# Attention scores as fp32r products over 128 rows of split queries and keys, and attention units in the order of heads

## The reference

```python
def diff_attend(q, k, v, lam):
    s = jnp.einsum('bhjqd,bhjkd->bhjqk', q, k).astype(jnp.float32) * (DA_HALF ** -0.5)
    p = jax.nn.softmax(s, axis=-1)
    w = p[:, :, 0] - lam * p[:, :, 1]
    return jnp.einsum('bhqk,bhkd->bhqd', w.astype(v.dtype), v)
...
    q_l = apply_rope(da_heads(dq), cos, sin)
    k_l = apply_rope(da_heads(dk), cos, sin)
    k_all = jnp.concatenate([k_l, k_c], axis=3)
```

## Time and profile before

| | |
|---|---|
| median of 3 runs | 2370.67 us (2369.45 to 2372.53) |
| profiled execution, its own time | 2370.8 us |
| its span, first to last instruction | 2369.0 us |
| TensorE busy | 2342.1 us, 99% of the span |
| VectorE busy | 1600.7 us, 68% |
| ScalarE busy | 978.1 us, 41% |
| mean granted TensorE clock | 0.999 |

### The profile page before, as it was taken

The page is one execution under the profiler, slowest core; times in us unless marked ns, Lnnn a source line. Parts: engine busy times, 40 slices in busy tenths (PEclk is TensorE's granted clock), DMA queues, the critical chain, the costliest instruction groups (busy, mean ns, idle before and its releaser), DMA issues.

```text
span 2369.0 us, 35156 instructions
## 1 busy us (share of the span) xinstructions
PE 2342.1 (99%) x12814; PEld 2014.8 (85%) x12814; DVE 1600.7 (68%) x2635; ACT 978.1 (41%) x1625; POOL 197.7 (8%) x186
## 2 busy tenths in 40 slices
PE   8999999999999999999999999999999999999998
PEld 5888889887887778898888898888898888999997
DVE  6998577456546445569885367887665756668876
ACT  5423224434345334363322254232245346555554
POOL 2111000000000000031111000211100000001220
PEclk9999999999999999999999999999999999999999
DMA  8888464232222322327883337775644433556654
GB/s 275 244 249 241 126 209 143 81 98 72 72 63 80 90 80 65 113 83 238 247 243 120 96 85 231 236 237 179 185 116 116 116 98 107 161 137 198 191 162 140
DMA packets 540054, 356.86 MB, mean 151 GB/s; under 512 B 15206, under 2 KB 490896, under 8 KB 539920
## 3 DMA queue, kind: packets, MB, share of 16 engines
q1 hardware_dynamic: 538472, 354.70, 51.0%
q10 hardware_dynamic: 1448, 0.38, 0.1%
HBM read 337.20 MB, written 17.83 MB: 150 GB/s over the span
## 4 chain that ended last, share of the span: by engine, by line
PE 91%; DVE 3%; ACT 2%; issue 2%; DMA 1%; SPq 1%; POOL 0%; DVEq 0%; ACTq 0%; POOLq 0%
PE ps L1015 25%; PE ps L1017 24%; PE ps L1016 24%; PE ps L1380 2%; PE ps L1314 2%; PE ps L1315 2%; PE ps L1313 2%; PE ps L1028 1%; PE ps L1395 1%; PE ps L1107 1%; PE ps L1109 1%; PE ps L1108 1%; PE ps L1356 1%; PE ps L1412 1%; PE ps L1030 1%
## 5 line engine op out<-in xcount | busy, mean ns | idle before, releaser
L2176 DVE TENSOR_TENSOR w_lo<-raw,w_hi 128x1024 fp32r<-128x1024 f32 (+3 forms) x430 | 496.2, 1155 | 480.0 <-ACT w_hi L1518 475.5
L1518 ACT ACTIVATE w_hi<-raw 128x1024 fp32r<-128x1024 f32 (+3 forms) x430 | 423.3, 985 | 895.6 <-PE ps L1017 714.1
L1015 PE MATMUL ps<-u_hi,w_hi 128*128 128x512 f32 (+2 forms) x2176 | 782.2, 359 | 1.7 <-DVE dav L2776 1.0
L1017 PE MATMUL ps<-u_hi,w_lo 128*128 128x512 f32 (+2 forms) x2176 | 772.6, 355 | 0.0
L1016 PE MATMUL ps<-u_lo,w_hi 128*128 128x512 f32 (+2 forms) x2176 | 772.3, 355 | 0.0
L1015 PEld LDWEIGHTS ps<-u_hi,w_hi 128*128 128x128 f32 x2176 | 410.9, 189 | 60.9 <-DVE dav L2776 1.8
L1017 PEld LDWEIGHTS ps<-u_hi,w_lo 128*128 128x128 f32 x2176 | 410.8, 189 | 58.2
L1016 PEld LDWEIGHTS ps<-u_lo,w_hi 128*128 128x128 f32 x2176 | 411.1, 189 | 55.9
L2592 DVE SCALAR_TENSOR_TENSOR ada_acc<-ada_in_up,cs,ada_acc 128x512 f32<-128x512 f32 x378 | 282.1, 808 | 0.0
L1015 PE MATMUL ps<-g,w_hi 128*128 128x512 f32 (+1 forms) x572 | 206.7, 361 | 0.0
L1017 PE MATMUL ps<-g,w_lo 128*128 128x512 f32 (+1 forms) x572 | 203.8, 356 | 0.0
(11 more groups left out here) (334 smaller groups left out, 3467.6 us busy)
## 6 DMA issues: line engine op xcount, KB each, us to landing
raw<-in_ffn_up SPq DMA_DIRECT2D x150, 512.0 KB, 4.7
raw<-in_w_in SPq DMA_DIRECT2D x132, 512.0 KB, 3.8
ada_in_up<-in_w_ada SPq DMA_DIRECT2D x108, 512.0 KB, 4.5
raw<-in_ffn_down SPq DMA_DIRECT2D x67, 384.0 KB, 3.3
fold_out<-ada_acc SPq DMA_DIRECT2D x32, 512.0 KB, 3.4
fold<-fold_out SPq DMA_DIRECT2D x32, 512.0 KB, 5.5
raw<-in_ffn_down SPq DMA_DIRECT2D x42, 320.0 KB, 3.1
h<-in_ffn_up SPq DMA_DIRECT2D x22, 512.0 KB, 4.5
```

Of the source, the lines that this page charges most:

```text
L1015: pe.matmul(ps[bank][:, cols_of], wh, a_hi, start=a, stop=False)
L1017: m = pe.matmul(ps[bank][:, cols_of], wl, a_hi, start=False, stop=b)
L1518: act.activation(hi, whole, ACT.Copy).then_inc(hi_done, 1)
L2176: dve.tensor_tensor(lo, whole, hi.bitcast(F32), ALU.subtract).then_inc(lo_done, 1)
```

## The change

The kernel after keeps, for one head at a time, split queries `qs` and keys `ks`. `qs[:, j, 0]` has the high part of half j's queries twice, in rows 0 to 63 and again in rows 64 to 127; `qs[:, j, 1]` the low part, twice. `ks[:, j]` has the high part of half j's keys in the 64 rows where they lie in `dqk` and their low part in the other 64. A score is then two fp32r products over 128 rows, accumulated in PSUM: high queries by both parts of the keys, low queries by both parts. To make these, ScalarE does 4 casts for a head's queries (`queries_high`) and 2 for its keys (`keys_high`), VectorE 4 and 2 subtractions (`queries_low`, `keys_low`), each over 64 partitions. The units go head by head, so that `qs` and `ks` can be written once for each head; the writes for the next head wait for the last scores of the one before (`head_free`). Head 0's queries are split in `proj_order` behind `ysplit` 5, its keys at the list's end, behind the last `dav`, because `ks` lies in the memory of `value_bias`.

```diff
-    order += [("dv", 1), ("rope", 3), ("rope", 7), ("ysplit", 4), ("ysplit", 5)]
+    order += [("dv", 1), ("rope", 3), ("rope", 7), ("ysplit", 4), ("ysplit", 5), ("queries", 0)]
     order += [("dv", 2), ("ysplit", 6), ("ysplit", 7), ("dv", 3)]
...
-    return [(head, t, range(2 if t < 2 else 4)) for t in tiles for head in range(HEADS)], 16 * layer
+    return [(head, t, range(2 if t < 2 else 4)) for head in range(HEADS) for t in tiles], 16 * layer
...
+    qs = at("qs", [P, 2, 2, TOK], F32R, 1152)
+    ks = at("ks", [P, 2, TOK], F32R, 1152 + 8192)
...
-            if v < HEADS:
-
-                pe.wait_ge(rope_done, 8 * layer + 2 * (head + 1))
+            if v % units_of_head(layer) == 0:
+                pe.wait_ge(q_ready, HEADS * layer + head + 1)
+                pe.wait_ge(k_ready, HEADS * layer + head + 1)
...
             for j in range(2):
-                half = slice(j * DA_HALF, (j + 1) * DA_HALF)
-                pe.matmul(ps[SCORE_BANK + j][:, 0:len(keys) * P], dqk[half, head, t * P:(t + 1) * P],
-                          dqk[half, 4 + head, 0:len(keys) * P], start=True, stop=True).then_inc(sc_ready, 1)
+                out, moving = ps[SCORE_BANK + j][:, 0:len(keys) * P], ks[:, j, 0:len(keys) * P]
+                pe.matmul(out, qs[:, j, 0, t * P:(t + 1) * P], moving, start=True, stop=False)
+                pe.matmul(out, qs[:, j, 1, t * P:(t + 1) * P], moving, start=False, stop=True).then_inc(sc_ready, 1)
...
+        def queries_high(layer, head):
+
+            t = slice(t0_of(layer), TOK)
+            act.wait_ge(rope_done, 8 * layer + 2 * (head + 1))
+            head_free(act, layer, head)
+            for j, own in enumerate(HALF_ROWS):
+                for rows_of in HALF_ROWS:
+                    m = act.activation(qs[rows_of, j, 0, t], dqk[own, head, t], ACT.Copy)
+            m.then_inc(q_high, 1)
+
+        def keys_high(layer, head):
+
+            if head == 0:
+                act.wait_ge(evac_dve, BASES[layer, "proj"][2] + PLANS[layer]["dv", 3][3] + 1)
+            head_free(act, layer, head)
+            for j, own in enumerate(HALF_ROWS):
+                m = act.activation(ks[own, j, :], dqk[own, 4 + head, :], ACT.Copy)
+            m.then_inc(k_high, 1)
...
+                    if step[0] == "scores" and next_head(layer, step[1]):
+                        queries_high(layer, next_head(layer, step[1]))
+                        keys_high(layer, next_head(layer, step[1]))
...
+        def queries_low(layer, head):
+
+            t = slice(t0_of(layer), TOK)
+            dve.wait_ge(rope_done, 8 * layer + 2 * (head + 1))
+            dve.wait_ge(q_high, HEADS * layer + head + 1)
+            for j, own in enumerate(HALF_ROWS):
+                for rows_of in HALF_ROWS:
+                    m = dve.tensor_tensor(qs[rows_of, j, 1, t], dqk[own, head, t], qs[own, j, 0, t].bitcast(F32),
+                                          ALU.subtract)
+            m.then_inc(q_ready, 1)
...
                     outputs(layer, step[1])
+                    if next_head(layer, step[1] + 1):
+                        queries_low(layer, next_head(layer, step[1] + 1))
+                        keys_low(layer, next_head(layer, step[1] + 1))
```

More of the change, by code:

```diff
@@ L245, in attention_units, with units_of_head, next_head @@
     tiles = range(2 if layer == DEPTH - 1 else 0, TT)
-    return [(head, t, range(2 if t < 2 else 4)) for t in tiles for head in range(HEADS)], 16 * layer
+    return [(head, t, range(2 if t < 2 else 4)) for head in range(HEADS) for t in tiles], 16 * layer
+def units_of_head(layer):
+    return len(attention_units(layer)[0]) // HEADS
+def next_head(layer, v):
+    n = units_of_head(layer)
+    return (v + 1) // n if (v + 1) % n == 0 and v + 1 < HEADS * n else None
 def gate_order(layer):
@@ L600, in build @@
     ng_split = sem("ng_split")
+    q_high, q_ready, k_high, k_ready = (sem(n) for n in ("q_high", "q_ready", "k_high", "k_ready"))
     ng_ready, s_ready, e_ready, pw_ready = (sem(n) for n in ("ng_ready", "s_ready", "e_ready", "pw_ready"))
@@ L667, in u32_of, with head_free @@
         return u32(n, ITEM_OF[k])[:, k % 2 * SEG:(k % 2 + 1) * SEG]
+    HALF_ROWS = (slice(0, DA_HALF), slice(DA_HALF, P))
+    def head_free(eng, layer, head):
+        if head:
+            units, u0 = attention_units(layer)
+            eng.wait_ge(sc_ready, 2 * (u0 + units_of_head(layer) * head))
+        else:
+            eng.wait_ge(ada_turned, (ADA_OF[1, "up0"] if layer else ADA_OF[0, "up1"]) - 4 +
+                        (ADA_UP + ADA_DOWN[1] if layer else 0))
     def run(eng, count, body, peel_first=False, peel_last=False):
@@ L888, in mixer @@
                         sp.wait_ge(*proj_done(layer - 1, CH_PROJ - 1))
+                        sp.wait_ge(sc_ready, 2 * len(attention_units(layer - 1)[0]))
                     for kind, n in (("mv", 2), ("dv", 1)):
@@ L1970, in mixer @@
                     split_y(y_number(layer, "mo", step[1]), ht[:, step[1], :], yml_hi, step[1], t0)
+                elif step[0] == "queries":
+                    queries_high(layer, 0)
+            keys_high(layer, 0)
             for step in GATE_ORDERS[layer]:
@@ L2879, in ml_numerator, with keys_low @@
                                      ALU.mult, ALU.add).then_inc(hsum_ready, 1)
+        def queries_low(layer, head):
[7 more added lines that the diff above has]
+            m.then_inc(q_ready, 1)
+        def keys_low(layer, head):
+            dve.wait_ge(k_high, HEADS * layer + head + 1)
+            for j, own in enumerate(HALF_ROWS):
+                m = dve.tensor_tensor(ks[HALF_ROWS[1 - j], j, :], dqk[own, 4 + head, :], ks[own, j, :].bitcast(F32),
+                                      ALU.subtract)
+            m.then_inc(k_ready, 1)
         def maxima(layer, v):
@@ L2990, in mixer @@
                     split_y(y_number(layer, "mo", step[1]), ht[:, step[1], :], yml_hi, yml_lo, step[1], t0)
+                elif step[0] == "queries":
+                    queries_low(layer, 0)
                 elif step[0] == "gates":
@@ L2996, in mixer @@
                     rope(layer, step[1])
+            keys_low(layer, 0)
             for step in GATE_ORDERS[layer]:
```

## The result

The changed kernel takes 2392.22 us (median of five runs, 2390.32 to 2395.49) beside 2370.9 us for the kernel before (five runs, 2369.45 to 2372.53): 0.91% slower, ratio 1.0091 with a 95% interval of 1.008 to 1.0102. The forecast was 2384 us. The measured time is 8.2 us above it and 1.2 us above the upper end of the range. The profiled execution of the changed kernel has 2390.67 us of its own and a span of 2388.9 us, 19.9 us more than before in both.

The account below looks back on a forecast made before the run. TensorE, busy 99% of the span, was taken to bound the kernel: -8.1 us from products, +13.5 at changes of head, +7.9 at gate-stage starts, +13.3 on 2370.8, giving 2384 us (0.56% slower), range 2374 to 2391 us.

Parts of the forecast that it names:

- products give back: Score products on TensorE: 0.33 us saved per wide unit, 0.35 per narrow one, 8.1 us in all.
- first gate chunk, layer 0: Start of layer 0's gate stage: TensorE waits 4.1 us for `dav`, delayed by head 0's query copies.
- unit 3 to 4: Change of head in layer 0: TensorE waits 3.6 us for the next head's split copies.
- unit 7 to 8: Change of head in layer 0, behind a whole chunk's split: TensorE waits 4.6 us for the copies.
- unit 11 to 12: Change of head in layer 0, with an `ml` chunk: TensorE arrives later and waits 1.8 us.
- first gate chunk, layer 1: Start of layer 1's gate stage: `dav` comes 2.3 us later behind the query copies, added to TensorE's 0.96 us wait.
- first scores, layer 1: Layer 1's first scores: head 0's key copies end after TensorE's 24 products, a wait of 1.5 us more.
- changes of head, layer 1: TensorE's waits for copies at layer 1's three changes of head: 1.3 us, 2.2 us and none.
- the clock: Rival: three waits of 3.6 us or more each bring a 1.2 GHz stretch costing 1.74 us; 2389.3 us, chance 0.17.
- the rival of 2376 us: Copies on neighbouring, different partitions overlap by 0.1 us each, making waits 8.0 us less; chance 0.15.
- products save nothing: Rival: two side-by-side float32 score products take as long as four fp32r ones; 2392.2 us, chance 0.05.
- What I called covered on VectorE: Next `w_lo` and maxima, about 4 us late behind the copies at changes of head, cost TensorE no wait.

Follow-up runs that it names:

- e7: Changed kernel with head 0's copies earlier at the gate stage's start, two key buffers and next queries copied tile by tile: 2365.97 us, ratio 0.9980.
- e2: Changed kernel with 512-column products that nobody reads filling TensorE's waits: 2384.63 us, ratio 1.0058.
- e5: Changed kernel with only the start of the gate stage reordered, head 0's queries and keys split earlier, `y` splits last: 2385.28 us, ratio 1.0062.
- e4: Changed kernel with all copies and its order, but scores again as two float32 products over 64 rows: 2402.22 us, ratio 1.0128.
- e1: Kernel before with only the order of units changed to head by head: 2371.26 us, ratio 0.9998.
- e9: As e7, but head 0's keys split later, casts behind the split at `dv` 2, subtractions behind the last `dav`: 2365.57 us, ratio 0.9975.
- e8: Changed kernel with VectorE's six subtractions for the next head directly behind the weights of a head's last unit: 2379.57 us, ratio 1.0031.
- e10: Changed kernel with the gate-stage start of e9 and the earlier subtractions of e8, no second key buffer: 2370.76 us, ratio 0.9996.
- e3: Changed kernel with only head 0's queries and keys split, other heads reading them, so output differs from the reference: 2372.79 us, ratio 1.0006.
- e6: Changed kernel with only the changes of head spread out: two key buffers, next head's queries copied tile by tile: 2373.23 us, ratio 1.0009.

## Why the forecast fell short

The predicted steps, beside what they measured:

| step | predicted us | measured us |
|---|---|---|
| products give back | 8.1 | 0.32 for a wide unit (0.33 predicted); 7.7 in e7, its waits for `dav` set aside |
| first gate chunk, layer 0 | 4.1 | 4.12 |
| unit 3 to 4 | 3.6 | 3.49 |
| unit 7 to 8 | 4.6 | 4.45 |
| unit 11 to 12 | 1.8 | 1.73 |
| first gate chunk, layer 1 | 2.3 more | 3.05 - 0.96 = 2.1 more |
| first scores, layer 1 | 1.5 | 0.36; 1.58 in e2, at full clock |
| changes of head, layer 1 | 1.3, 2.2, 0 | 1.15, 2.11, none |
| the clock | 0 in the sum | at most 7.75 (windows); 7.6 or 6.3 (e2, medians or spans) |

**The step that failed is the clock.** I had it as a rival with a chance of 0.17, at 1.74 us for each of three waits and at 2389.3 us, and left it out of the sum, which put it at nothing. The runs show it in the changed kernel (four windows below 1.00) and its price in e2 (6.3 us by the spans, 7.6 by the medians). With it the working comes out: -8.1 + 19.5 of waits + 7.75 at most is +19.2 us, against 19.9 in the profiled execution; by layers -5.4 + 13.8 + 4.3 = 12.7 (measured 12.5) and -2.6 + 5.7 + 3.4 = 6.5 (measured 6.6), the clock's share being the windows' again. The median lies still 1.4 us further out than that execution. That execution's granted clock is 0.995, and that of the others goes with their times: 0.995 at 2390.32 us, 0.994 at 2392.22 and 2394.54, 0.993 at 2395.49. So the clock's price differs from one execution to the next.

**How the rival was mis-sized.** Three waits of 3.6 us or more, one stretch each, was the guess. The clock fell behind four waits: 4.12, 4.45, the 3.05 at 2020.01, and the 2.11 at 2071.16, which I had thought too short. Behind 3.49 us at 784.30 it did not fall, while at the same place it did in e5 behind 3.49 us again, and in e4 behind 3.12. And behind 4.45 us the loss was 0.35 x 8 = 2.8 us, more than one stretch's 1.74. So the number of falls can't be read from the length of the waits alone, but it was wrong to give the rival less than a half when the forecast's own waits were its condition. The Trainium skill, in TensorE: Matmul & The Clock Gate, section Why this matters for your kernels, advises against idle gaps between bursts of products. These rows bear it out in the main, with the 1.00 at 784.00 as the exception.

**The first scores of layer 1** are no second error. Predicted was a wait of 1.5 us, TensorE waited 0.36. TensorE's 24 products, begun at 2020.01, ran partly at the 1.2 GHz level (the window from 2016 has 0.83) and so were through at 2024.37, 4.4 us later instead of 3.0. A wait was exchanged for slower products: in e2, where the clock stayed up, the 1.58 us are there. So some 1.2 us of the windows' 7.75 replaced a wait, and what the clock added is nearer to 6.5 us, beside the 6.3 that e2's span gave back.

**What was right, and shown.** The copies, which change partitions each time, don't overlap: 2.78 us for four, 1.39 for two; this decides against the rival of 2376 us. The products do give back 8 us, by the unit's rows in the change and in e4, and by e7; with the rival "products save nothing" (2392.2 us, which the result happens to equal) e7 could not have been faster than before. A time that agrees with a rival says nothing for it while its mechanism is absent. The order of the units is free (e1). What I called covered on VectorE was nearly covered in the change (waits for `w_lo` of 1.3 us in all, 0.7 before). Where the copies stand elsewhere it was not: in e9 TensorE waits 2.0 us for `w_lo`, and in e8 and e10 the turned weights come late.

**What stays open:** why the clock holds behind one wait and falls behind another of the same length or a shorter one. The twelve traces of this case, the program's first wait left out, have 26 waits of TensorE of 2 us or more, and the clock fell behind or within 20 of them, among these all 8 that were longer than 4 us; of the 16 between 1 and 2 us it fell at two (1.78 us in e4, 1.90 in e1). No run was made to vary the length of one wait by itself; the last section has a place where it varied unasked.

## What to carry to other kernels

A faster product that needs its operands prepared is worth what it gives back less what TensorE waits for the preparation; here 8.1 us against 19.5, and it pays (0.2%) only with a second buffer and an earlier place in the queues together, which take the preparation off the path. On a kernel that keeps TensorE busy without a break, price each new wait of 2 us or more with a stretch at the 1.2 GHz level on top, here 1.5 to 2.8 us each, and take that as the likely case: 20 of 26 such waits had one here. When a queued instruction is moved ahead, look one engine further: what waited behind it on its own queue may be what holds up the next one.

## Not expected of the hardware

The granted clock fell behind surprisingly short waits, and not always. In e1, whose only edit lies 600 us later, TensorE had a wait of 1.90 us for POOL's `fold` at 84.65 where the kernel before had one of 1.41 us (84.52). The windows of e1 and of the kernel before, the same 7 us:

```profile
85.00:92.00 7.00, 7.00 (x25) 5.54 (x25) 7.00 (x11) 1.28 (x2) 0.00 (x0) 0.76 0.73 194
```

```profile
85.00:92.00 7.00, 7.00 (x33) 5.77 (x32) 7.00 (x12) 1.61 (x3) 0.00 (x0) 1.00 0.78 208
```

25 products instead of 33, and a granted clock of 0.76: 1.7 us lost, which is a third of what the kernel's measurement can tell from no change. The order of instructions ahead of this place is the same in all kernels of this case, so nothing that an experiment tests sets this wait, and it shows one wait at many lengths:

| wait at 84 to 86 us | the clock behind it |
|---|---|
| 1.41 (before), 1.46 (e7), 1.50 (e2), 1.63 (e10), 1.70 (after) | holds |
| 1.90 (e1) | falls |
| 2.02 (e5), 2.38 (e3) | holds |
| 2.38 (e8), 2.50 (e4), 2.69 (e6), 3.54 (e9) | falls |

The longer the wait, the likelier a fall, but 2.38 us went both ways. A single profiled execution can so differ from the next of the same kernel by a fall's 1.7 us that no edit has made.
